# Mixture-of-experts kernel: the sixth weight buffer moved to dead tiles, the residual rows kept on chip, and the last two units reordered

## The reference

```
h = _rmsnorm(x, norm_ffn)
# 4 groups of 8 experts: best group, then the best 2 experts inside it
gu = einsum('td,edf->tef', h, w_gu);  g_act, up = split(gu, 2)     # 32 experts, 1024 -> 2 x 256
act = silu(g_act) * up * combine
x = x + einsum('tef,efd->td', act, w_dn)                            # 256 -> 1024
return _rmsnorm(x, norm_final)
```

## Time and profile before

| | us |
|---|---|
| median of 3 runs | 1184.95 |
| the profiled execution's own time | 1186.36 |
| its span | 1184.6 |
| TensorE busy in the span | 1116.2 (94%) |
| VectorE busy | 538.4 (45%) |
| ScalarE busy | 351.5 (30%) |
| GpSimd busy | 117.3 (10%) |

### The profile page before, as it was taken

How to read it: one execution, slowest core, us unless ns; L and a number is a source line. 1 busy time by engine, 2 the same in 40 slices (tenths; PEclk the granted TensorE clock), 3 DMA queues, 4 the chain that set the end, 5 groups by cost and what they waited for, 6 DMA issues and landing times.

```text
span 1184.6 us, 16485 instructions
## 1 busy us (share of the span) xinstructions
PE 1116.2 (94%) x6487; PEld 615.4 (52%) x6487; DVE 538.4 (45%) x1199; ACT 351.5 (30%) x676; POOL 117.3 (10%) x148
## 2 busy tenths in 40 slices
PE   6999999999999899988799999999999999999777
PEld 6545744444744589875465444456653333333223
DVE  6876333324399635596672222235442212121117
ACT  4114631111676423203664100165301111111004
POOL 2000012221000000001010000022111111111000
PEclk9999999999999899999989999999999999999889
DMA  8111022131113443330034000446388999999988
GB/s 285 37 57 56 14 82 69 64 97 50 36 36 134 190 129 84 132 144 1 3 141 178 0 1 1 148 173 236 117 290 342 413 390 421 421 424 421 423 322 353
DMA packets 67894, 204.74 MB, mean 173 GB/s; under 512 B 24573, under 2 KB 41185, under 8 KB 57313
## 3 DMA queue, kind: packets, MB, share of 16 engines
q1 hardware_dynamic: 61104, 186.64, 41.4%
q0 software_dynamic: 6656, 16.95, 3.8%
q10 hardware_dynamic: 48, 0.01, 0.0%
HBM read 171.58 MB, written 37.24 MB: 176 GB/s over the span
## 4 chain that ended last, share of the span: by engine, by line
PE 73%; DVE 10%; DMA 5%; issue 3%; ACT 3%; POOL 0%; SPq 0%; DVEq 0%; POOLq 0%; ACTq 0%
PE bank L2674 20%; PE bank L1583 11%; PE bank L1639 8%; PE bank L1606 5%; PE bank L1701 2%; PE bank L1654 2%; DMA arena<-in_w_e_gu 2%; DMA arena<-x_d 2%; PE bank L2801 2%; PE bank L805 1%; PE bank L916 1%; PE bank L1960 1%; PE bank L1569 1%; PE bank L866 1%; PE bank L853 1%
## 5 line engine op out<-in xcount | busy, mean ns | idle before, releaser
L2674 PE MATMUL bank<-arena 128*128 128x512 f32 (+3 forms) x1032 | 358.0, 506 | 8.1 <-ACT arena L2178 6.8
L2674 PEld LDWEIGHTS bank<-arena 128*128 128x128 f32 x1032 | 196.9, 192 | 163.0 <-issue 140.7
L1583 PE MATMUL bank<-arena 128*32 128x512 f32 x1344 | 150.4, 599 | 8.3 <-issue 7.3
L1583 PEld LDWEIGHTS bank<-arena 128*32 128x32 f32 x1344 | 44.8, 111 | 109.4 <-issue 109.4
L1639 PE MATMUL bank<-arena 128*128 128x512 f32 x220 | 95.6, 592 | 0.0
L2178 ACT ACTIVATE arena<-bank 128x512 f32<-128x512 f32 (+1 forms) x57 | 28.4, 504 | 167.3 <-PE bank L2674 166.8
L1606 PE MATMUL bank<-arena 128*32 128x512 f32 x672 | 76.5, 595 | 1.4 <-ACT arena L1246 1.4
L1356 DVE TENSOR_TENSOR arena<-arena,bank 128x256 f32<-128x256 f32 x21 | 8.9, 422 | 149.4 <-ACT arena L1242 149.4
L1399 DVE TENSOR_TENSOR arena<-arena,bank 128x512 f32<-128x512 f32 x32 | 22.0, 688 | 100.2 <-PE bank L1639 79.5
L1639 PEld LDWEIGHTS bank<-arena 128*128 128x128 f32 x220 | 41.3, 190 | 49.7 <-issue 49.7
L1242 ACT ACTIVATE arena<-bank 128x256 f32<-128x256 f32 x21 | 8.1, 383 | 156.7 <-PE bank L1583 156.7
(11 more groups left out here) (408 smaller groups left out, 1564.2 us busy)
## 6 DMA issues: line engine op xcount, KB each, us to landing
arena<-in_w_e_gu SPq DMA_DIRECT2D x27, 2048.0 KB, 13.2
arena<-in_w_e_dn SPq DMA_DIRECT2D x32, 1024.0 KB, 13.5
arena<-in_w_in SPq DMA_DIRECT2D x11, 1024.0 KB, 5.2
arena<-y_d SPq DMA_DIRECT2D x8, 1024.0 KB, 11.1
arena<-hz_d SPq DMA_DIRECT2D x4, 1792.0 KB, 8.0
pk_d<-arena SPq DMA_DIRECT2D x8, 640.0 KB, 2.9
hz_d<-arena SPq DMA_DIRECT2D x4, 1280.0 KB, 4.9
arena<-in_w_e_gu SPq DMA_DIRECT2D x5, 1024.0 KB
```

The source lines that it names most:

```text
L1583: ins = mm(bank[part, :], hgT[:, k, part], w_gu(buf(es[i]), k), start=(k == 0), stop=(k == KT - 1))
L2674: ins = mm(psum[PROJ_BANKS[u % 3]][0:rows, 0:n], lhs(k), rhs(k), start=(k == 0), stop=(k == kt - 1))
```

## The change

1. **Buffers.** `triu`, `triu_s`, `tril_s`, `head_ones`, `levT`, `lru_w`, `memk` and `memv` become slices of one tile, `early`, of 3072 columns. Nothing in it is used any more once the units run. `arena` grows by 2048 columns at its end. The gate and up weights of buffer 5 go to `early` (6 of 8 pieces) and to the last 1024 columns of the old arena (2 of 8), so each such load is now two DMAs. Its down weights go to the 2048 new columns. The space comes from the scratch of GpSimd's DMAs: 8192 bytes per partition.
2. **Residual.** `x2` stays where it is. The eight stores, the load back and all waits on them are gone. The tail reads `x2[:, m]` in place of `xb[m]`, and the tail's other tiles move to free places.
3. **Waits.** The load of expert 5 waits for 6 counts of `t_r_dve` in place of 4, and still for the first gather. The load of the final norm's weights (`fin_g`) waits until the gate and up products of unit 20 are made.
4. **Order.** Unit 19's `act_tr` and `down` run ahead of the gate and up products of unit 20 on TensorE. ScalarE and VectorE follow: they empty unit 19's down products before they work on unit 20's gates.

The diff, cut to what carries this (the rest renames tiles and places):

```diff
-        arena = sb("arena", [48024])
+        arena = sb("arena", [48024 + 2 * D])
...
-                 ((o_g3, 0, 4), (o_tmp + 6 * D, 4, 6), (o_cx, 6, 8)), ((o_bc, 0, KT),)]
-        DN_AT = [o_g2 + GU, GU, EW + GU, o_g1 + GU, o_g1 + EW, o_bc + GU]
+                 ((o_g3, 0, 4), (o_tmp + 6 * D, 4, 6), (o_cx, 6, 8)), ((None, 0, 6), (48024 - 1024, 6, 8))]
+        DN_AT = [o_g2 + GU, GU, EW + GU, o_g1 + GU, o_g1 + EW, 48024]
+        piece = lambda off, n: early[:, 0:n] if off is None else arena[:, off:off + n]
...
-                sp.wait_ge(s["rms_r"], G3 + m + 1)
-                sp.dma_start(x2_d[m], x2[:, m]).then_inc(s["t_x2"], 16)
                 sp.wait_ge(s["t_xn"], 16 * (m + 1))
...
-            sp.wait_ge(s["t_r_dve"], 4)
-            sp.wait_ge(s["t_x2"], X2_STORED)
+            sp.wait_ge(s["t_r_dve"], 6)
             sp.wait_ge(moe["g0"], 16)
             load_gu(sp, 5)
             load_dn(sp, 5)
             sp_experts(sp, moe, 0)
-            sp.wait_ge(moe["dn"], UN - 2)
-            x2_back(sp)
...
             for u in range(UN + 1):
+                if u == UN - 1:
+                    act_tr(u - 1)
+                    down(u - 1)
                 if u < UN:
                     gate_up(u)
-                if u >= 1:
+                if u >= 1 and u != UN - 1:
                     act_tr(u - 1)
                 if u + 1 < UN:
                     tr(u + 1)
-                if u >= 1:
+                if u >= 1 and u != UN - 1:
                     down(u - 1)
...
             pe.wait_ge(moe["y"], 2 * UN)
-            pe.wait_ge(s["t_x2"], X2_BACK)
             for m in range(4):
                 start(m)
...
+            sp.wait_ge(moe["gu"], UN)
-            sp.dma_start(fin_g, a["norm_final"].unsqueeze(0).to_broadcast([P, D])).then_inc(s["x_row"], 16)
+            sp.dma_start(fin_g, a["norm_final"].unsqueeze(0).to_broadcast([P, D])).then_inc(s["t_x2"], 16)
             pass_end(sp, moe, 0)
...
-    nc = bacc.Bacc("TRN2", target_bir_lowering=False, num_devices=1)
+    nc = bacc.Bacc("TRN2", target_bir_lowering=False, num_devices=1, dynamic_dma_scratch_size=8192)
```

More of the change, by code:

```diff
@@ L44, in hybrid_trunk @@
         ones = sb("ones", [P])
[L45 to L49, removed]
+        early = sb("early", [3072])
+        triu, triu_s, tril_s, head_ones = [early[:, i * P:(i + 1) * P] for i in range(4)]
+        levT = early[:, 512:1536].rearrange("p (a b) -> p a b", a=NL + 1)
+        lru_w = early[:, 1536:2048].rearrange("p (a b) -> p a b", a=2 * CT)
         negmask = sb("negmask", [P])
@@ L112, in hybrid_trunk @@
         slot = lambda c: (c - 6) % KT
-        memk = sb("memk", [CT, ML])
-        memv = sb("memv", [MT_, GW])
+        memk = early[:, 2048:2560].rearrange("p (a b) -> p a b", a=CT)
+        memv = early[:, 2560:3072].rearrange("p (a b) -> p a b", a=MT_)
         bf_tm = sb("bf_tm", [NT, NH])[:, :, :]
@@ L1015, in hybrid_trunk @@
         over_i = kp(1).bitcast(i32)
-        rx = region(o_tmp + 7168, 48024)
-        b_rank, b_hit = rx(NRO, NBL), rx(NRO, NBL)
+        rw = region(48024 - 1024, 48024)
+        rx = region(o_tmp + 7168, 48024 - 1024)
+        b_rank, b_hit = rw(NRO, NBL), rx(NRO, NBL)
         b_rank_i = b_hit.bitcast(i32)
-        toks_of = [rx(BT * TK, NE) for _b in range(2)]
+        toks_of = [rw(BT * TK, NE) for _b in range(2)]
         slotT = rx(P)
@@ L1050, in hybrid_trunk @@
         actT = view(o_tmp + 5 * D + 3 * FE, FE // P, P)
[L1051 to L1056, removed]
+        yg = [view(i * TK * D, TK, D) for i in range(6)] + [view(o_g2 + i * TK * D, TK, D) for i in range(2)]
+        y_out = [view(o_g1 + i * D, D) for i in range(NT)]
+        fin_g = view(o_g3, D)
+        w_diag = view(o_g2 + 5 * D, NT, P)
         xn_d = nc.dram_tensor("xn_d", (T, D), f32, kind="Internal").ap()
         y_d = nc.dram_tensor("y_d", (TK * T, D), f32, kind="Internal").ap()
-        x2_d = nc.dram_tensor("x2_d", (NT, P, D), f32, kind="Internal").ap()
-        X2_STORED = 16 * (1 + NT)
-        X2_BACK = X2_STORED + 32
         moe = ({n: s["e_" + n] for n in
@@ L1237, in act_experts, with gates @@
         def act_experts(act, q, p):
+            def gates(u):
+                act.wait_ge(q["gu"], UN * p + (u + 1))
+                after(act, q["ac"], UN * p, u)
+                nc.scalar.activation(sg, psum[2 + 4 * (u % 2)][:, 0:FE], ACT.Silu).then_inc(q["sg"], 1)
             for u in range(UN + 1):
[L1239 to L1242, removed]
+                if u < UN - 1:
+                    gates(u)
                 if u >= 1:
@@ L1350, in dve_experts, with gated @@
             tokens(0)
+            def gated(u):
+                dve.wait_ge(q["sg"], UN * p + (u + 1))
+                after(dve, q["at"], UN * p, u - 1)
+                v.tensor_tensor(actv[:, u % 2], sg, psum[2 + 4 * (u % 2)][:, FE:2 * FE], ALU.mult).then_inc(q["ac"], 1)
             for u in range(UN + 1):
                 b = u % 2
[L1353 to L1356, removed]
+                if u < UN - 1:
+                    gated(u)
                 if u + 1 < UN:
@@ L1983, in act_tail3 @@
                     scaled(act, m - 4)
-                link(nc.scalar.activation(junk, xb[m], ACT.Square, accum_out=ss[:, c]))
+                link(nc.scalar.activation(junk, x2[:, m], ACT.Square, accum_out=ss[:, c]))
                 nc.scalar.activation(rms[:, c], ss[:, c], ACT.Sqrt, bias=epsc[:, 0:1],
```

25 lines of the change are left out of this document (9 added, 16 removed).

## The result

The changed kernel took 1189.52 us (median of 18 runs, 1184.85 to 1194.58), the kernel before 1186.70 us on the same chip (18 runs, 1182.94 to 1189.81). The ratio is 1.0026, 95% interval 1.0016 to 1.0036: 3.1 us slower by the ratio (2.8 by the medians), where 3.5 us were predicted. The profiled execution has a span of 1188.7 us, against 1184.6.

A forecast was written before the change was run, and what follows sets the result against it. From 1105 on the weight stream, not TensorE, was taken to set the time. Last down products +6.9 us, a quicker scatter making the request +4.5, tail -1.0: +3.5 in all, 1188.5 us, range 1180.5 to 1192.

The forecast's parts named there:

- Place and cause: Ahead of unit 19's down products: TensorE idles 6.6 us until the down weights of experts 28 and 29 land at 1129.2.
- Clock: Behind the gap ahead of unit 19's down products: TensorE's lowered clock costs 2.0 us, bounds 0 to 2.2.
- Exposed chain: After unit 20's gate and up products: silu, gating, transposes, copy and down products, no longer hidden, take 5.8 us together.
- Last scatter: Before the expert rows' request: with the load back gone the scatter takes 4.3 us, against 6.66 before.
- Rival B: Last scatter no quicker, its 6.66 us being the scatter itself: +6.9 us, 1191.8; chance 0.17.
- Tail: From the expert rows' request to the end, 36.3 us before: 1.0 us gained, bounds 0 and 2.
- Stores, buffers, waits: Removed residual stores, split buffer 5 loads and the new wait for six counts: costed at nothing.
- A: Unit 19's down weights have landed by 1123.3, so the new order fills a wait: 4.4 us faster, 1180.6; chance 0.15.
- C: Freed residual traffic moves the weight stream, and the gap before unit 19 vanishes: 1173.1; chance 0.04.
- D: The change moves nothing that is timed; reorder stalls less, load back was hidden behind the last scatter: 1185; chance 0.08.
- two large terms: The stall from the new order, last down products +6.9 us, and the quicker last scatter, 4.3 us against 6.66.
- the load back's removal: Before the expert rows' request: the scatter gets the DMA engines nearly to itself, 4.3 us in place of 6.66.

The follow-up runs named there:

- e3: Changed kernel, with SyncE asking for the down weights of experts 28 and 29 before the gate and up weights of 30 and 31; ratio to kernel before 0.9993.
- e4: Changed kernel plus 7 extra matmuls, output unused, filling the gap ahead of unit 19's down products; ratio to kernel before 1.0010.
- e1: Changed kernel's buffers and on-chip residual, with the order of all units as in the kernel before; ratio to kernel before 0.9957.
- e2: Kernel before with only the new order of units 19 and 20, residual stores and load back kept; ratio to kernel before 1.0028.
- e5: Same kernel as e1 run again on a second chip, as base for others; ratio to kernel before 0.9972.
- e6: e1 with the eight residual stores made again while the router runs, nothing loaded back; ratio to kernel before 0.9971.
- e8: e1 with only unit 19's activation transposes moved ahead of unit 20's gate and up products, down products left behind them; ratio to kernel before 0.9954.
- e9: Same kernel as e8 run again on a third chip; ratio to kernel before 0.9949, median 1180.89 us against 1185.63.
- e10: e9 plus unused extra matmuls, 5 ahead of unit 19's and 4 ahead of unit 20's gate and up products; ratio to kernel before 0.9950.
- e7: e6 with the residual also loaded back into free memory, TensorE not waiting for it; ratio to kernel before 0.9994.

## Why the prediction was right

**Place and cause.** The predicted gap of 6.6 us ahead of unit 19's down products measured 6.99, and ended with the landing of down weights. The landing was taken at 1129.2, near the middle of bounds that two rows gave (1128.0 and 1130.2); it came at 1129.75. Only the lower bound rests on a landing, that of the load back; that it came so near the middle was in part luck. e3 shows that it is the order of SyncE's queue: with the same bytes in the other order this gap is gone, and a shorter one of 3.73 us stands ahead of unit 20.

**Clock.** 2.0 us were taken; 5.24 in place of 3.64 is 1.6 in the trace, and e4 gives 1.9 us by the ratios, whose intervals overlap, and 1.5 by the traces.

**Exposed chain.** 5.8 us were taken from the end of unit 20's gate and up products to that of the last down products; it took 5.8 (1141.95 to 1147.73). The last down products were predicted to end at 1147.5, and ended at 1147.7.

**Last scatter.** 4.3 us were taken from the first gather, 4.09 was measured, and 4.1 to 4.4 in e1, e2, e3, e5, e6, e8 and e9 (4.82 in e4, 3.45 in e10). Rival B (the scatter itself takes 6.66) needed over 6.2 and falls; e7 shows it the other way round. The estimate of 3.2 us that the Trainium skill gives ("DMA: Bandwidth & Descriptors", section on the anatomy of one DMA) was about 1 us too short in eight of these ten traces, and by 0.3 us in e10; here a trace of a like transfer was the better price.

**Tail.** 1.0 us of gain was taken, 0.5 measured (36.3 to 35.8). The first tiles do start as predicted, at their landing (idle 1.29 and 0.43 us, released by `y_d`), and SyncE issues the last stores 31.8 us after the request, where before it was 32.9 (1181.2 - 1148.3). But from there to the end of the span it takes 4.0 us in place of 3.4. This is the term that was mis-sized. The prediction followed VectorE's chain up to the last stores and took what lies behind for unchanged. SyncE's last wait, for the landing of these stores, is 2.6 us in place of 1.9, which covers the 0.6 us. Why they land later was not tested.

**Stores, buffers, waits.** Costed at nothing; e6 agrees for the stores, within the 1.9 us it can tell, and e1 and e5 show no cost of the rest. Rivals A and C fall with the gap, D with e1 and e2: both parts move the time, in opposite directions.

What the prediction did not say is that its two large terms depend on each other. It put -2.4 us down to the load back's removal, and e2 shows that the same 2.3 us come from the stall alone. In this term the attribution was wrong and the number right: with both edits made, the scatter is quick for either reason.

The prediction also gave 0.69 to a time that could not be told from the kernel before, taking 0.5% for what a measurement can tell. The interval came out at 0.1% on either side, and 3.1 us is clear of it. Measured from unit 19's start the two traces give 3.8 us (76.6 to 80.4); the 0.7 us between that and the ratio are not explained.

## What to carry to other kernels

When a kernel waits for a stream of loads, as this one does, moving work ahead of a wait pays only if the work's own operands stand ahead in the queue: read the issue order of the loads before the order of the products is changed, and move what needs no load (e8) or reorder the loads with it (e3). A wait that the profile shows for a transfer may be free while the transfer is paid for elsewhere, so ask which other transfer shares the engines at that moment. Two edits near one stall are not to be added up: time each alone.

## What the runs showed of the hardware

- In these traces the clock fell after a gap as short as 2.2 us, and in some executions only. In e5 unit 20's products came after 2.17 us idle and took 8.78 us in place of 7.1, with this clock:

```profile
1122.72 8.78 PE L1565 MATMUL bank<-arena 128*32 128x512 f32 x64 [2.17 <-issue]
```

```profile
1123.00:1125.00 2.00, 2.00 (x20) 0.71 (x16) 0.00 (x0) 0.00 (x0) 0.00 (x0) 0.76 0.94 393
1125.00:1127.00 2.00, 2.00 (x16) 0.62 (x12) 0.00 (x0) 0.00 (x0) 0.00 (x0) 0.50 0.82 332
```

  By single microseconds it was still 1.00 from 1123 to 1124, with TensorE busy throughout, and 0.52 from 1124 to 1125: it fell behind the gap, when the products had been running for over a microsecond. In e6, after 2.44 us idle, it fell about a microsecond behind the start of the products in the same way (8.77 us). The same code after 2.31 us idle (e1) and unit 20 after 3.73 us (e3) ran at full clock. The length of the gap alone does not decide it.
- The last scatter of 128 rows of 4 KB took 4.1 to 4.4 us from its start to the request behind it in eight of the ten traces in which the load back had landed or was gone (4.82 in e4 and 3.45 in e10, both unexplained), and 6.66 and 6.68 us in the two in which the load back was landing on another queue.
- The full weight stream runs at 424 GB/s in both kernels (1060 to 1110 us of the changed one); the load issued into it at 1096.25 landed 33.5 us later.
- In the tail the transfers and not TensorE seem to set the end. In the ten traces in which TensorE waits for the expert rows of the last tile, the span ends 10.3 to 10.4 us after it starts on them (1178.30 to 1188.7 in the changed kernel, 1176.08 to 1186.5 in e6). No run tests it.
